# Hybrid decoder step: when the first recurrent weight blocks are loaded, when the last head's sums are prepared, and at which point the gates stand

## The chip, the cores and the metric

The kernel runs on one core of a Trainium2 chip. The metric is the device time of one execution in microseconds (us). Engines are named as in the profile: PE (TensorE matmul), PEld (its weight loads), DVE (VectorE), ACT (ScalarE), POOL (GpSimd), SP (SyncE, which here only issues DMAs).

## What is computed

One layer of a decoder for 512 prompt rows and 8 samples of 8 rows, 576 rows in all, of width 2048, in float32:

```
mod = silu(c) @ w_ada + b_ada                      # six vectors of 2048 for each condition
hn = rmsnorm(x, g1) * (1 + sc1) + sh1
q, k, v, xl, gl = split(hn @ w_in)                 # 8 heads of 128; xl, gl of 1024
attn = stick_breaking(q, k, v, bias)               # samples also over 8 cached pages of 128 keys each
xc = causal_conv4(xl)
r, i = sigmoid(xc @ w_a + b_a), sigmoid(xc @ w_x + b_x)    # 8 diagonal blocks of 128
a = exp(-8 * r * softplus(-lam)); h[t] = a[t] * h[t-1] + sqrt(1 - a[t]^2) * i[t] * xc[t]
x = x + gt1 * (concat(attn, h * gelu(gl)) @ w_out)
x = x + gt2 * conv_ffn(rmsnorm(x, g2) * (1 + sc2) + sh2)   # w_up 2048x12288, conv 3, gelu, w_down
```

Stick-breaking weights are exp(log_sigmoid(z) + sum of log_sigmoid(-z) over the later keys). Each sample attends to its own 8 new rows and to its 1024 cached rows.

## The kernel before

Everything stands transposed, features on the partitions and the 576 rows along the free dimension, as two halves of 288. Each float32 weight is split into a high and a low part (`hi` on ACT, `lo` on DVE), and a product of one **weight block** (1024 input rows by 128 output columns, 512 KB) is 48 matmuls of 288 columns (L713). Blocks pass through four slots `raw`, `w_hi`, `w_lo`: SP loads `raw` (`load`, L494), ACT makes `w_hi` (L1218), DVE `w_lo` (L1692), PE uses them. Each engine's program is one fixed list; the engines meet only by counters (`wait_ge`), so an instruction that waits holds up all behind it on its engine. The same is so on SP, whose DMAs are issued in order: a load that waits for its buffer keeps back all later ones.

The layer runs in stages:

- **Heads.** For head i, PE makes q, k and v in six block products. Between them stand five **modulation chunks** (`ada_chunk`, SP's L556, PE's L729: 1 MB of `w_ada` in two DMAs through the ring `ada_q`, whose slots come free as PE uses the chunk two before) and the work of the head before: `scores` (L809), `sums` (the sums over later keys, L821 and L826), `turn_kv`, and `weigh` (the product with the values, L843). The logits go through ACT (Abs, Exp, Ln) and DVE; `sums` needs their softplus `sp_` split again, into `high` by ACT (`sums_high`, L1275) and `low` by DVE (`sums_low`, L1789, into memory that the profile calls `ops`).
- **First recurrent block.** `lru_block(0, 0..3)`, four block products (two for xl, two for gl), stand among the last head's `scores(NH)`, `sums(NH)` and `weigh(NH)`. Behind `sums(NH)` PE sums the samples' own keys (L1011, L1015), which waits for `self_sp_ready`: the logits of the samples against their own rows, made by DVE (L1972, semaphore `self_z`), through ACT's Abs, Exp, Ln (L1437 to L1439, semaphore `self_exp`) and back on DVE (L1982 to L1984).
- **Points.** The cached keys and values, 64 pages each of 512 KB, are worked off at 128 **points** (i, p), p from 0 to 15. A point with a key page has eight transposes (L911, L915), whose results ACT and DVE copy to SBUF (L1413 and L1925, `left_taken` and `right_taken`), and eight small matmuls (`score`, L926), which work on the page of the point before and so need its copies. A point with a value page has eight small matmuls (`weigh_page`, L959). The sixteen points of round i = 0 stand alone. In the rounds 1 to 7 they stand between the matmuls of the four products `lru_block(i, q)`, one for every two of the eight input tiles.
- **Gates.** In round i, PE makes the gates of recurrence i - 1 (`gates(i - 1)`, L895: two matmuls for r, two for i). Both pass through the PSUM banks 0 and 1, which the products of xl and gl use too. So PE first waits for gl (`gl_out`, ACT's Gelu L1378), makes r, does a point, waits until ACT has read r (`r_taken`, Sigmoid L1384), makes i, does another point, waits until ACT has read i (`i_taken`), and begins the products. ACT then makes the coefficients (L1360, L1361), DVE `recurrence_a` (L1861 to L1864), ACT the root (L1365), DVE `recurrence_b` (two scans), and ACT may take the next xl only after that (`lru_done`).
- **Output projection and feed-forward.** PE takes 16 + 16 blocks of `w_out`, 48 tiles of `w_up` (L1113) and 8 groups of `w_down` (L713).

In what order SP, ACT and DVE reach these steps is written out by hand: SP in the loop over b (`ada_chunk`, then `qkv_block(b + LEAD)` with LEAD = 6), ACT and DVE in loops `for p in range(16)` with `if p == ...`. POOL loads the pages through four buffers.

In head 7 (the last), SP's loop has no more q, k and v blocks to load, and the first block of the recurrent products is issued after all five modulation chunks.

## Time and profile before

| what | value |
|---|---|
| median of 3 runs | 3016.62 us (3013.79 to 3017.61) |
| the profiled execution | 3015.11 us, its span 3013.3 us |
| PE busy | 2880.0 us, 96% of the span |
| PEld busy | 2726.0 us, 90% |
| DVE, ACT, POOL busy | 59%, 40%, 10% |
| mean granted TensorE clock | 0.982 of full speed |
| heads | up to about 580 us of the span |
| first recurrent block | about 580 to 632 us |
| points of round 0; rounds 1 to 7 | about 632 to 667 us; 667 to 1020 us |
| output projection; feed-forward | to about 1270 us; to the end |

A line of the profile names the source line, the engine, the operation and what it writes and reads. "Idle" in square brackets is the time in which the engine stood before that instruction, with what ended it. Times of a timeline count from the first instruction. The granted clock is a share of TensorE's full 2.4 GHz; 0.50 is its lower level, 1.2 GHz.

### The profile page before, as it was taken

What the parts mean: (1) busy time and instruction counts of PE and PEld (TensorE: products, weight loads), DVE (VectorE), ACT (ScalarE), POOL (GpSimd) and SP (SyncE); (2) the same over time, 40 slices, a digit from 0 to 9 for tenths busy, and PEclk for the clock granted to TensorE, in tenths of its full rate; (3) what the DMA queues carried; (4) which work ended last, traced back from release to release, by engine and by line L of the source; (5) the groups of instructions that cost most, each with busy time, mean ns of one, the idle gap of its engine ahead of it and who ended that gap; (6) DMA issues with size and microseconds to landing.
All of it is one profiled execution on the core that took longest, in us unless ns stands there. A gap on an engine that the chain in (4) does not pass through costs nothing.

```text
span 3013.3 us, 60900 instructions
## 1 busy us (share of the span) xinstructions
PE 2880.0 (96%) x24110; PEld 2726.0 (90%) x24110; DVE 1764.5 (59%) x2738; ACT 1216.5 (40%) x1481; POOL 293.6 (10%) x545
## 2 busy tenths in 40 slices
PE   6799999879999999969999999999999999999999
PEld 2499999868888899869999999999999999999999
DVE  0433343344444432398888888888888755555553
ACT  1345555444444421254444444444444422222222
POOL 0000000011212100011111111111111100000000
PEclk9799999989999999979999999999999999999999
DMA  9966555455766697523333333333333633333323
GB/s 336 338 168 171 162 162 141 141 160 177 228 201 212 191 250 220 143 69 111 103 112 104 113 109 97 111 109 111 111 95 114 206 108 108 103 106 107 105 81 107
DMA packets 608837, 444.53 MB, mean 148 GB/s; under 512 B 14553, under 2 KB 556111, under 8 KB 607453
## 3 DMA queue, kind: packets, MB, share of 16 engines
q1 hardware_dynamic: 584630, 353.39, 40.2%
q0 software_dynamic: 23904, 84.15, 8.9%
q10 hardware_dynamic: 144, 4.72, 0.4%
q8 instruction: 118, 1.93, 0.3%
q14 instruction: 41, 0.34, 0.0%
HBM read 408.14 MB, written 34.06 MB: 147 GB/s over the span
## 4 chain that ended last, share of the span: by engine, by line
PE 86%; DVE 5%; ACT 4%; DMA 3%; issue 1%; SPq 0%; POOL 0%; ACTq 0%; DVEq 0%; POOLq 0%
PE ps L713 40%; PE ps L1113 35%; PE ps L729 2%; DMA wide<-in_w_ada_dram 2%; PE ps L911 1%; PE ps L926 1%; PE ps L791 1%; DMA ada_o<-in_w_ada_dram 1%; PE ps L809 1%; PE ps L737 1%; PE ps L959 1%; PE ps L763 1%; PE ps L843 1%; PE ps L915 1%; ACT w_hi L1218 1%
## 5 line engine op out<-in xcount | busy, mean ns | idle before, releaser
L1113 PE MATMUL ps<-ops,w_hi 128*128 128x288 f32 x4608 | 920.4, 296 | 1.5 <-DVE w_lo L2076 1.5
L1113 PEld LDWEIGHTS ps<-ops,w_hi 128*128 128x128 f32 x4608 | 742.0, 189 | 1.7 <-DVE w_lo L2076 1.7
L1113 PE MATMUL ps<-ops,w_lo 128*128 128x288 f32 x2304 | 679.5, 295 | 0.0
L1692 DVE TENSOR_TENSOR w_lo<-raw,w_hi 128x1024 fp32r<-128x1024 f32 x240 | 294.0, 1225 | 647.6 <-ACT w_hi L1218 646.5
L713 PE MATMUL ps<-gs,w_hi 128*128 128x288 f32 x3072 | 534.0, 296 | 0.0
L1218 ACT ACTIVATE w_hi<-raw 128x1024 fp32r<-128x1024 f32 x240 | 253.6, 1057 | 679.1 <-PE ps L713 649.9
L713 PEld LDWEIGHTS ps<-gs,w_hi 128*128 128x128 f32 x3072 | 452.4, 189 | 0.0
L1113 PEld LDWEIGHTS ps<-ops,w_lo 128*128 128x128 f32 x2304 | 437.9, 190 | 0.0
L713 PE MATMUL ps<-act_hi,w_hi 128*128 128x288 f32 x1792 | 403.4, 307 | 18.4 <-DVE act_lo L1756 13.5
L713 PE MATMUL ps<-act_hi,w_lo 128*128 128x288 f32 x1792 | 385.1, 297 | 0.0
L713 PE MATMUL ps<-act_lo,w_hi 128*128 128x288 f32 x1792 | 384.7, 297 | 0.0
L713 PE MATMUL ps<-gs,w_lo 128*128 128x288 f32 x1536 | 329.1, 296 | 0.0
L713 PEld LDWEIGHTS ps<-act_hi,w_hi 128*128 128x128 f32 x1792 | 286.7, 190 | 44.4 <-issue 29.9
L713 PEld LDWEIGHTS ps<-act_lo,w_hi 128*128 128x128 f32 x1792 | 290.4, 190 | 0.0
L713 PEld LDWEIGHTS ps<-act_hi,w_lo 128*128 128x128 f32 x1792 | 290.1, 190 | 0.0
L1520 ACT ACTIVATE w_hi<-ax 128x1024 fp32r<-128x1024 f32 x144 | 152.9, 1061 | 260.4 <-PE ps L1113 254.7
L713 PEld LDWEIGHTS ps<-gs,w_lo 128*128 128x128 f32 x1536 | 247.6, 189 | 0.0
L2076 DVE TENSOR_TENSOR w_lo<-raw,w_hi 128x1024 fp32r<-128x1024 f32 x168 | 205.5, 1223 | 53.4 <-ACT w_hi L1520 53.3
L1520 ACT ACTIVATE w_hi<-raw 128x1024 fp32r<-128x1024 f32 x168 | 177.4, 1057 | 109.2 <-PE ps L1113 105.0
L2076 DVE TENSOR_TENSOR w_lo<-ax,w_hi 128x1024 fp32r<-128x1024 f32 x144 | 175.7, 1220 | 31.9 <-ACT w_hi L1520 31.9
L1113 PE MATMUL ps<-op,w_hi 128*128 128x288 f32 x768 | 157.5, 300 | 29.1 <-DVE ops L2168 29.1
L2212 DVE SCALAR_TENSOR_TENSOR uc<-up,vec,uc 128x592 f32<-128x592 f32 x192 | 159.9, 833 | 12.7 <-DVE uc L2212 6.4
(353 smaller groups left out, 3218.4 us busy)
## 6 DMA issues: line engine op xcount, KB each, us to landing
raw<-in_w_up_dram SPq DMA_DIRECT2D x120, 512.0 KB, 4.3
raw<-in_w_down_dram SPq DMA_DIRECT2D x128, 384.0 KB, 3.3
raw<-in_w_in_dram SPq DMA_DIRECT2D x80, 512.0 KB, 4.5
ada_q<-in_w_ada_dram SPq DMA_DIRECT2D x80, 512.0 KB, 5.4
wide<-in_w_ada_dram SPq DMA_DIRECT2D x32, 1024.0 KB, 11.2
page<-in_cache_k_dram POOLq DMA_DIRECT2D x64, 512.0 KB, 4.6
page<-in_cache_v_dram POOLq DMA_DIRECT2D x64, 512.0 KB, 4.5
ada_o<-in_w_ada_dram SPq DMA_DIRECT2D x48, 512.0 KB, 6.5
```

What stands on the lines that cost most here:

```text
L713: mm = pe.matmul(out[:, h, :], w[s][:, kk, :], x[:, row, h * HALF:(h + 1) * HALF], start=first and kk == kks[0] and w is w_hi and x is hi, ...
L729: mm = pe.matmul(ps[32 * j:32 * j + CW, bank, R0:R0 + P], cs[:, h * KB + kk, :], ring[:, slot, kk, :], start=False, stop=h == 1 and kk >= ...
L737: mm = pe.matmul(ps[:, bank, 448 + CB * j:448 + CB * (j + 1)], rows[:, j, :], sel[:], start=True, stop=True)
L763: mm = pe.matmul(ps[:, 1 + h, 0:HALF], neg_ones, sq[:, k % 2, h * HALF:(h + 1) * HALF], start=first, stop=last)
L791: mm = pe.matmul(ps[32 * j:32 * j + CW, bank, :], cs[:, WK * q + j, :], wide[:, (b + 4) % WIDE, j, :], start=q == 0, stop=q == 3, skip_gro ...
L809: pe.matmul(ps[:, b, c:c + QW[j]], kf[:, j * P:(j + 1) * P], qf[:, j * P:SEQ], start=True, stop=True)
L1113: mm = pe.matmul(ps[:, bank, 0:HALF], w[slot][:, kk, :], moving(i, kk, low), start=i not in ADDED and kk == 0 and w is w_hi and not low, s ...
L1218: act.activation(w_hi[s][:], raw[s][:], ACT.Copy).then_inc(hi_done, 1)
L1520: act.activation(w_hi[n % SLOTS if isinstance(n, int) else (7 * jj + i) % SLOTS][:], weight(j, jj, i)[:], ACT.Copy) \
L1692: dve.tensor_tensor(w_lo[s][:], raw[s][:], w_hi[s][:].bitcast(F32), ALU.subtract).then_inc(lo_done, 1)
L2076: dve.tensor_tensor(w_lo[slot][:], weight(j, jj, i)[:], w_hi[slot][:].bitcast(F32), ALU.subtract).then_inc(lo_done, 1)
L2212: dve.scalar_tensor_tensor(uc[which][:], up[which][:, w:w + SEQ + NB * 10], col, uc[which][:], ALU.mult, ALU.add).then_inc(done, 1)
```

## The change

Three things are written in another place; no instruction is added or taken out.

1. SP: the blocks 0 to 5 of the recurrent products (those of `lru_block(0, 0..3)` and two of `lru_block(1, ...)`) are loaded in the loop over b, each behind the modulation chunk of its b, as the q, k and v blocks are; blocks 6 and 7 follow, and the loop begins at i = 2.
2. The last head: ACT's `sums_high(NH)` stands behind `take_v(NH)`, ahead of `hi(u, 5)` and of the Abs, Exp, Ln of the samples' own keys; DVE's `sums_low(NH)` stands right behind the instruction that signals `self_z`, ahead of `lo(u, 5)` and of the rest of that chain.
3. Gates: in each round i of 1 to 7, PE does points 0 and 1, then gate r, point 2, gate i, point 3, and the first product has two points inside, after its fourth and sixth input tile. ACT takes the gates at p = 2 and 3, and DVE's `recurrence_a` comes at p = 4.

```
--- before.py
+++ after.py
@@ sync engine: weight blocks and modulation chunks
+            def lru_block(n):
+                i, k = n // 4, n % 4
+                load(turn(B_LRU, i, 4), k, wi_v, KB * (k % 2), KB, 128 * i + 3072 + 1024 * (k // 2))
             for b in range(LEAD):
                 qkv_block(b)
             sp.wait_ge(sem("x_turned"), KT)
...
                 if b + LEAD < 6 * NH:
                     qkv_block(b + LEAD)
+                else:
+                    lru_block(b + LEAD - 6 * NH)
+
+            for n in range(LEAD, 8):
+                lru_block(n)
 
             def lru(i):
...
-            turns(sp, NL, lru)
+            with sp.Fori(2, NL) as i:
+                lru(i)
@@ tensor engine: points inside a recurrent block's product
                 def between(kk):
-                    if kk in (2, 4, 6) and points:
-                        point(i, points[kk // 2 - 1])
+                    if kk in (6, 4, 2)[:len(points)]:
+                        point(i, points[len(points) - 1 - (6, 4, 2).index(kk)])
@@ tensor engine: gates
                 gate(i, 0, "r_mm")
-                point(i + 1, 1)
+                point(*((i + 1, 2) if i + 1 < NL else (NL, 0)))
                 if i + 1 < NL:
                     pe.wait_ge(sem("r_taken"), i + 1)
                 gate(i, 1, "i_mm")
...
             for i in range(1, NL):
                 point(i, 0)
+                point(i, 1)
                 gates(i - 1)
-                point(i, 2)
+                point(i, 3)
                 pe.wait_ge(sem("i_taken"), i)
-                lru_block(i, 0, (3, 4, 5))
+                lru_block(i, 0, (4, 5))
                 lru_block(i, 1, (6, 7, 8))
@@ scalar engine
             take_v(NH)
+            sums_high(NH)
             hi(u, 5)
...
             act.activation(wsl, wsl, ACT.Ln, bias=1.0).then_inc(sem("self_exp"), 1)
-            sums_high(NH)
             hi(u, 6)
...
-                    if p in (1, 2):
-                        take_gate(i - 1, p - 1)
+                    if p in (2, 3):
+                        take_gate(i - 1, p - 2)
@@ vector engine
                                      ALU.mult, ALU.add).then_inc(sem("self_z"), 1)
+            sums_low(NH)
             lo(u, 5)
...
             dve.tensor_tensor(z3, wsl.rearrange("p (h q) -> p h q", q=SAMP), same3, ALU.mult).then_inc(sem("self_sp_ready"), 1)
-            sums_low(NH)
             dve.memset(xlp[:, 0:3], 0.0)
...
-                    if p == 3:
+                    if p == 4:
                         recurrence_a(i)
```

The order of the instructions shows this at three places. On SP, in the last head and the first recurrent block (L556 is a modulation chunk's half, L494 a weight block), before:

```order
L494 DMA raw<-in_w_in_dram 128x8x128 x2
L556 DMA ada_q<-in_w_ada_dram 128x8x128 x10
L494 DMA raw<-in_w_in_dram 128x8x128 x4
L87 UNCONDITIONAL_BRANCH
L87 ISA
```

and now:

```order
L556 DMA ada_q<-in_w_ada_dram 128x8x128 x2
L494 DMA raw<-in_w_in_dram 128x8x128
L556 DMA ada_q<-in_w_ada_dram 128x8x128 x2
L494 DMA raw<-in_w_in_dram 128x8x128 x4
L586 UNCONDITIONAL_BRANCH
L586 ISA
```

The first two rows of the new piece are the last of four such pairs. Each of the first blocks moved ahead of the modulation chunks that used to stand before it.

On ACT, from the last head's values to its weights (`high` is `sums_high`, the `La` rows are the samples' own keys), before:

```order
L1293 ACTIVATE vn<-ps 128x512
L1218 ACTIVATE w_hi<-raw 128x1024
L1437 ACTIVATE La<-X 64x512
L1438 ACT_TABLE_LOAD
L1438 ACTIVATE La<-La 64x512
L1439 ACT_TABLE_LOAD
L1439 ACTIVATE La<-La 64x512
L1275 ACTIVATE high<-X 128x1280
```

and now:

```order
L1303 ACTIVATE vn<-ps 128x512
L1285 ACTIVATE high<-X 128x1280
L1228 ACTIVATE w_hi<-raw 128x1024
L1448 ACTIVATE La<-X 64x512
L1449 ACT_TABLE_LOAD
L1449 ACTIVATE La<-La 64x512
L1450 ACT_TABLE_LOAD
L1450 ACTIVATE La<-La 64x512
```

`high` moved ahead of a weight block and of the three steps of the own keys.

On PE, at the head of round 1 (xc, wg are the gates; kt is a `score`; page a transpose of a key page), before:

```order
L915 MATMUL ps<-ident,page 128x128 x4
L895 MATMUL ps<-xc,wg 128x288 x2
L926 MATMUL ps<-kt,X 32x128 x8
L911 MATMUL ps<-ident,page 128x128 x4
L915 MATMUL ps<-ident,page 128x128 x4
L895 MATMUL ps<-xc,wg 128x288 x2
L926 MATMUL ps<-kt,X 32x128 x8
L911 MATMUL ps<-ident,page 128x128 x4
L915 MATMUL ps<-ident,page 128x128 x4
L713 MATMUL ps<-act_hi,w_hi 128x288 x2
```

and now:

```order
L924 MATMUL ps<-ident,page 128x128 x4
L935 MATMUL ps<-kt,X 32x128 x8
L920 MATMUL ps<-ident,page 128x128 x4
L924 MATMUL ps<-ident,page 128x128 x4
L904 MATMUL ps<-xc,wg 128x288 x2
L935 MATMUL ps<-kt,X 32x128 x8
L920 MATMUL ps<-ident,page 128x128 x4
L924 MATMUL ps<-ident,page 128x128 x4
L904 MATMUL ps<-xc,wg 128x288 x2
L935 MATMUL ps<-kt,X 32x128 x8
L920 MATMUL ps<-ident,page 128x128 x4
L924 MATMUL ps<-ident,page 128x128 x4
```

Both gates moved behind one more point, and the product (L722 in the new program) begins behind the last row.

## Rows read from the trace of the kernel before

**Rows 1.** Page: the chain that ended last, by engine

```profile
PE 86%; DVE 5%; ACT 4%; DMA 3%; issue 1%; SPq 0%; POOL 0%; ACTq 0%; DVEq 0%; POOLq 0%
```

**Rows 2.** PE's waits, whole span: waiter, releaser: total us, times, longest

```profile
PE ps L895 <- ACT La L1384: 12.4, 7, 5.4
...
PE ps L821 <- DVE ops L1789: 12.1, 2, 6.9
...
PE ps L926 <- DVE kt L1925: 6.7, 7, 1.3
...
PE ps L809 <- DVE mod L1697: 2.7, 1, 2.7
...
PE ps L895 <- ACT gg L1378: 1.7, 6, 0.4
```

**Rows 3.** The chain in order of time: start us, us, what

```profile
460.20 2.16 PE ps L843 x8
...
515.24 2.16 PE ps L843 x8
...
546.37 7.11 DMA raw<-in_w_in_dram
...
577.91 2.17 PE ps L843 x8
```

**Rows 4.** SP's timeline in the last head: start us, us, what was issued

```profile
498.99 47.33 SPq L556 DMA_DIRECT2D ada_q<-in_w_ada_dram  x10
```

**Rows 5.** ACT's and DVE's timelines, the last head's sums and the own keys

```profile
609.28 0.64 ACT L1437 ACTIVATE La<-X 64x512 f32<-64x512 f32 x1 [3.55 <-DVE X L1972]
...
613.71 1.25 ACT L1275 ACTIVATE high<-X 128x1280 fp32r<-128x1280 f32 x1
...
606.44 0.90 DVE L1783 TENSOR_TENSOR X<-X,before 128x128 f32<-128x128 f32 x4
...
615.34 0.68 DVE L1984 TENSOR_TENSOR X<-La,same 64x512 f32<-64x512 f32 x1
615.95 1.48 DVE L1789 TENSOR_TENSOR ops<-X,high 128x1280 fp32r<-128x1280 f32 x1
...
625.29 0.90 DVE L1804 TENSOR_TENSOR X<-X,before 128x128 f32<-128x128 f32 x4 [1.34 <-ACT X L1287]
```

**Rows 6.** PE's timeline of the same stretch

```profile
617.57 0.76 PE L821 MATMUL ps<-high,neg_later 128*128 128x512 f32 x1 [6.93 <-DVE ops L1789]
...
621.87 0.43 PE L1011 MATMUL ps<-neg_ones,X 128*32 128x1 f32 x32
...
629.71 2.32 PE L843 MATMUL ps<-X,vn 128*128 128x512 f32 x8
```

**Rows 7.** Stretches: us, busy (instructions) by engine, granted clock, DMA share, GB/s

```profile
592.00:597.00 5.00, 5.00 (x14) 3.15 (x13) 0.72 (x2) 0.00 (x0) 0.00 (x0) 0.52 0.35 105
645.00:668.00 23.00, 21.07 (x325) 15.97 (x318) 9.37 (x14) 7.62 (x13) 6.88 (x13) 1.00 0.82 282
879.60:884.70 5.10, 5.08 (x84) 3.83 (x84) 0.00 (x0) 1.19 (x2) 0.00 (x0) 0.67 0.80 259
```

**Rows 8.** PE's timeline: second gate (L895) of rounds 1 to 5, one score (L926)

```profile
676.51 2.29 PE L895 MATMUL ps<-xc,wg 128*128 128x288 f32 x4 [5.44 <-ACT La L1384]
...
732.11 1.24 PE L895 MATMUL ps<-xc,wg 128*128 128x288 f32 x4 [1.70 <-ACT La L1384]
...
780.26 1.24 PE L895 MATMUL ps<-xc,wg 128*128 128x288 f32 x4 [1.37 <-ACT La L1384]
...
827.64 1.24 PE L895 MATMUL ps<-xc,wg 128*128 128x288 f32 x4 [0.16 <-ACT La L1384]
...
839.64 0.43 PE L926 MATMUL ps<-kt,X 128*32 128x128 f32 x8 [0.87 <-DVE kt L1925]
...
879.62 1.90 PE L895 MATMUL ps<-xc,wg 128*128 128x288 f32 x4 [1.86 <-ACT La L1384]
```

**Rows 9.** ACT's timeline, rounds 1 and 3

```profile
674.42 1.28 ACT L1384 ACT_TABLE_LOAD   x1
...
776.62 0.59 ACT L1417 ACTIVATE wT<-ps 128x512 f32<-128x512 f32 x1
```

More of the change, by code:

```diff
@@ L572, in _ @@
                     qkv_block(b + LEAD)
+                else:
+                    lru_block(b + LEAD - 6 * NH)
+            for n in range(LEAD, 8):
+                lru_block(n)
             def lru(i):
@@ L577, in lru @@
                 tile(u, 2, wi_v, 128 * i + 4096)
-            turns(sp, NL, lru)
+            with sp.Fori(2, NL) as i:
+                lru(i)
             def out_block(b):
@@ L900, in between @@
                 def between(kk):
-                    if kk in (2, 4, 6) and points:
-                        point(i, points[kk // 2 - 1])
+                    if kk in (6, 4, 2)[:len(points)]:
+                        point(i, points[len(points) - 1 - (6, 4, 2).index(kk)])
                 product(turn(B_LRU, i, 4), q, gps[0], act_hi, act_lo, first=q % 2 == 0, last=q % 2 == 1, k0=KB * (q % 2),
@@ L1027, in gates @@
                 gate(i, 0, "r_mm")
-                point(i + 1, 1)
+                point(*((i + 1, 2) if i + 1 < NL else (NL, 0)))
                 if i + 1 < NL:
@@ L1036, in _ @@
                 point(i, 0)
+                point(i, 1)
                 gates(i - 1)
[L1038 removed]
+                point(i, 3)
                 pe.wait_ge(sem("i_taken"), i)
[L1040 removed]
+                lru_block(i, 0, (4, 5))
                 lru_block(i, 1, (6, 7, 8))
@@ L1432, in _ @@
             take_v(NH)
+            sums_high(NH)
             hi(u, 5)
@@ L1439, in _ @@
             act.activation(wsl, wsl, ACT.Ln, bias=1.0).then_inc(sem("self_exp"), 1)
-            sums_high(NH)
             hi(u, 6)
@@ L1973, in _ @@
                                      ALU.mult, ALU.add).then_inc(sem("self_z"), 1)
+            sums_low(NH)
             lo(u, 5)
```

12 lines of the change are left out of this document (6 added, 6 removed).

## The prediction

> **What bounds the kernel now.** First the shares of the chain that ended last: PE holds 86% of it [rows 1]. So nothing is won by making ACT, DVE or a transfer shorter as such; only time in which PE stands, or runs at its lower clock, can be got back. The second view is PE's own waits over the whole span [rows 2]. Those that the change can touch are these: L895 (the gates) on ACT's La, 12.4 us in 7 times; L821 (the sums) on DVE's L1789, 12.1 us in 2; L926 (scores) on DVE's kt, 6.7 us in 7. The third is the chain in order of time [rows 3], where a period shows that a head is late. The last is the granted clock of short stretches [rows 7]: after a wait of some us PE works for a while at 1.2 GHz instead of 2.4, so a wait costs more than its own length.
>
> All three edits lie before 1020 us of the span, in code that each engine runs as a fixed list. What stands behind (output projection, feed-forward) waits for no clock time of its own, and I let it shift as it is.
>
> **Part 1, the first recurrent blocks.** `weigh` (L843) of one head follows that of the head before by 515.24 - 460.20 = 55.04 us, and in the last head by 577.91 - 515.24 = 62.67 us [rows 3]. The difference is 7.6 us. Its cause: SP spends 47.33 us, from 498.99 on, in ten halves of modulation chunks [rows 4], the last of which waits for PE to free a slot, and only then, at 546.37, issues the first recurrent block, which lands 7.11 us later [rows 3]. ACT's `sums_high` stands behind `hi` of that block, DVE's `sums_low` behind it, PE's sums behind that: the shorter of the two L821 waits, 12.1 - 6.9 = 5.2 us [rows 2]. The other 2.4 us are the lower clock afterwards. With the change SP's order in this head is that of the head before, so the period should be 55.04 too. What is moved costs SP's queue nothing that PE sees: a block now waits on DVE's counter ahead of the next modulation chunk, exactly as a q, k or v block does in the other heads, and PE shows no wait for a chunk of `ada_q`. What is late next: nothing, by the pattern of the head before. **7.6 us**; the lower end is the bare wait, 5.2.
>
> **Part 2, the last head's sums.** PE stands 6.93 us before L821 at 617.57 [rows 6], that is from 610.6 on. DVE finishes `sp_` at 606.44 + 0.90 = 607.3, but ACT copies it to `high` only at 613.71, behind the own keys' chain, and DVE's 1.48 us come at 615.95 [rows 5]. With the change ACT copies from 607.4 to 608.7 (1.25 us, rows 5), DVE does its part when it has signalled `self_z` (ACT's start at 609.28 dates that) and is done at about 610.8, so PE's wait is all but gone. But right behind these sums PE needs `self_sp_ready`. That comes from the own keys' chain, which runs from 609.28 to L1984's end at 616.0 [rows 5]; ACT now starts it one weight block later, about 0.3 us, so it ends at 616.3. **So a new wait takes the place of the old one**: the sums need at most 621.87 - 617.57 = 4.3 us, PE is through by 615.1 at the latest (some 1.4 us sooner at full clock) and stands until 616.4. L1011 comes at 616.4 instead of 621.87 [rows 6]. `weigh` was 629.71 - 621.87 = 7.8 us later, so 624.2; it also needs `w_ready`, at 625.29 + 0.90 = 626.2 before [rows 5]. DVE's list up to it is 1.5 us shorter by the moved L1789 and 0.3 later: 625.0 to 625.1. So `weigh` starts at 625.1 instead of 629.71: 4.6 us.
>
> From this goes a price for the clock. PE now stands about 2.7 us in front of L1011. The nearest row is a wait of just that length (L809, 2.7 us [rows 2]), and behind it the clock was 0.52 over 5 us [rows 7], which is 5 x 0.48 = 2.4 us lost. Of those, 625.1 - 624.2 = 0.9 are under the wait for `w_ready`. I take the clock as lowered: 4.6 - 1.5 = **3.1 us**; the ends are 3.1 and 4.6.
>
> **Part 3, the gates.** PE's order is the same in the seven rounds, what stands late is not. A key point takes PE about 1.5 us at full clock, a value point 0.6.
>
> - Round 1: PE stands 5.44 us before the second gate [rows 8]. ACT is in the softplus of sixteen pages until 674.42, then loads a table, does La (ends 676.5) and only then copies kt [rows 9]. Now the copy for point 1 stands ahead of the table load, at 674.4 to 675.0, and PE does point 2 from there while ACT makes La. It starts again at 675.05 instead of 676.51: 1.5 us. The gate's own wait is covered by point 2, which at the lower clock takes PE 3 us.
> - Round 2: a wait of 1.70 [rows 8], now with point 2 (1.5) in it. But point 3 holds values, 0.6 us, and ACT's second sigmoid takes 0.3 longer than that: 1.70 - 0.2 - 0.35 = 1.15.
> - Round 3: 1.37 [rows 8], and 0.4 for gl. Here point 1 follows the turning of weights at point 0, and its transposes need ACT's copy wT, done at 776.62 + 0.59 = 777.2 [rows 9], so PE stands there about 0.9 instead, and then 0.85 for La. Gain 0.35.
> - Rounds 4 and 6: 0.16 for La [rows 8] and 0.17 for gl each, all covered now: 0.6 together.
> - Round 5: 1.86, and the gate takes 1.90 instead of 1.24 us [rows 8], because the clock falls: over 5.1 us it is 0.67 [rows 7], 1.6 us lost. The wait is split in two of about 0.8 (the copy wT; the sums that DVE takes from PSUM), each shorter than those after which the clock stayed (1.70). Gain 0.6 + 1.6 = 2.2.
> - Round 7: what the seven La waits leave, 12.4 - 5.4 - 1.7 - 1.4 - 0.3 - 1.9 = 1.7, and 0.4 for gl; four value points, as uncovered as in round 3: 0.5.
> - DVE's `recurrence_a` used to keep the copy of point 4 back, and PE waited for it at 839.64, 0.87 us [rows 8]. It stands behind that copy now. This holds for rounds 4 and 6; in round 1 it is the sixteen pages' sums that kept a copy back, and they start earlier. 3 x 0.9 = 2.7 of the 6.7 us [rows 2].
>
> The sum is 1.5 + 1.15 + 0.35 + 0.6 + 2.2 + 0.5 + 2.7 = **9.0 us**. What could be late next is `lru_done`, on which ACT's take of xl hangs: but `recurrence_b` starts behind DVE's copy of point 7, at the same place of PE's products as before, so its deadline does not move. Bounds: 4 us (what the two direct effects, rounds 1 and 2 and the copies, give with half of it lost to new waits) and 11.
>
> **A rule weighed.** At the stretch of round 0, where PE does nothing but transposes and small matmuls, the clock is 1.00 over 23 us [rows 7]. The Trainium skill says otherwise (TensorE: Matmul & The Clock Gate, Part 4: PE-mode transpose): transposes do not count as PE activity as other matmuls do, and the full clock does not engage for them. By the row, standing three or four points together costs nothing; by the rule it is a rival, below. The trace speaks against the rule.
>
> **The rivals.**
>
> - A. The gates' waits only move. ACT's list is unchanged in length, and every score or transpose of points 1 to 3 hangs on an ACT copy behind a table load. For it: rounds 3 and 7, where I find the same waits again under other names. Against: rounds 1 and 2, where real work fills them. Part 3 would give 1 us: 3016.6 - 7.6 - 3.1 - 1 = 3004.9.
> - B. The clock falls at other places. It fell behind waits of 1.86 [rows 8] and 2.7 us [rows 2] and stayed behind one of 1.70 [rows 8]; the waits shift by 8 to 20 us and may meet it differently. Each fall costs or returns about 2.4 us: 2991 to 3002 around the forecast; two falls more give 3001.6.
> - C. Slower. In the seven rounds PE now does points 0 to 3 and two gates in one piece, 5 to 7 us without a product. If the clock falls in such a piece and stays low as long as it did in rows 7 (5 us), each round loses 2.4 to 3 us, and the low clock runs on into the product. That decides once it happens in every round and lasts double: 7 x 5 = 35 us against 20 gained, 3032. Below four rounds in seven it is no loss. The 1.00 of round 0 speaks against it, and that PE in the old order too did three points and two gates in a piece of 5 us, where the clock fell only behind waits. By the Trainium skill's rule weighed above it would be so.
> - D. The change doesn't do what it says on SP: the blocks are early but the chunks come late, PE waits for `ada_q` once or twice for 2 to 3 us. Part 1 would give 4: 3000.4. The head before has the same order, with its transfers competing in the same way, and no such wait; its 55.04 us [rows 3] contain it.
>
> **How the numbers follow.** 7.6 + 3.1 + 9.0 = 19.7 us. The profiled execution took 3015.11 us, its span 3013.3; it would take 2995.4, with a span of 2993.6. The median of the runs shown is 1.5 us above it, so the forecast for the median is 3016.6 - 19.7 = 2996.9. Chances: the forecast with its own bounds, B within them, 0.78; A 0.12; D 0.05; C 0.02; something else without gain 0.03. The bounds of the parts give 5.2 + 3.1 + 4 = 12.3 to 7.6 + 4.6 + 11 = 23.2, so 2993.4 to 3004.3; with one fall of the clock more or less, and 1 us for the scatter of runs, and not the whole of each at once: 2991.0 to 3004.0. A's middle lies just outside, its better half inside. This kernel's measurement can tell 0.2%, 6 us, from no change: faster means below 3010.6, and the cases above it are C and the rest: faster 0.94, same 0.04, slower 0.02.
>
> **What would show each step.** Part 1: no wait before the last head's first L821, and 55 us between its `weigh` and that of the head before. Part 2: the wait before the second L821 under 0.5 us, a new one of 2 to 3 us before L1011, `self_sp_ready` as releaser, and a clock near 0.5 behind it; if the clock stays 1.00 there, add 1.5 us of gain. Part 3: gate waits for La of 2 to 3 us in all instead of 12.4; new waits for wT or kt before points 1 and 2 in rounds 1, 3, 5 and 7; waits of L926 for kt down from 6.7 to about 4; clock 1.00 in round 5. Wrong I would be by new waits of PE on `ada_q`, by a clock under 0.9 in rounds 2 to 7, or by a different time of the feed-forward, which should stay within 1 us.

## The result, and the profile after

| | before | after |
|---|---|---|
| median | 3015.3 us (4 runs, 3013.79 to 3017.61) | 2989.74 us (4 runs, 2988.73 to 2990.45) |
| the profiled execution | 3015.11 us, span 3013.3 | 2988.73 us, span 2987.0 |
| mean granted clock | 0.982 | 0.982 |

The ratio is 0.9917, with a 95% interval of 0.9905 to 0.9929: the kernel is 25.6 us faster. The forecast was 19.7 us and 2996.9 us, with a range from 2991.0. The measured median lies 1.3 us outside.

All lines below L713 stand some lines lower in the kernel after: L713 is L722 there, L809 L818, L821 L830, L843 L852, L895 L904, L911 L920, L926 L935, L1011 L1020; on ACT L1370 is L1380 and L1384 L1394. First the chain that ended last, by engine [rows 1]:

```profile
PE 88%; DVE 5%; ACT 3%; DMA 2%; issue 1%; SPq 0%; POOL 0%; ACTq 0%; DVEq 0%; POOLq 0%
```

PE's share of it is two per cent larger. Next PE's waits between 440 and 1030 us of the span (waiter, releaser: total us, times, longest), which answer to [rows 2]:

```profile
PE ps L935 <- ACT kt L1423: 7.3, 3, 3.6
PE ps L935 <- DVE kt L1935: 4.5, 6, 1.3
...
PE ps L818 <- DVE mod L1707: 2.7, 1, 2.7
PE ps L1020 <- DVE X L1995: 2.5, 1, 2.5
PE ps L920 <- ACT wT L1427: 2.0, 2, 1.0
PE ps L904 <- ACT La L1394: 1.3, 2, 0.8
PE ps L968 <- ACT wT L1427: 1.0, 1, 1.0
PE ps L961 <- DVE psp L1928: 0.8, 1, 0.8
...
PE ps L722 <- ACT Lb L1394: 0.5, 2, 0.3
...
PE ps L830 <- DVE ops L1799: 0.2, 1, 0.2
```

The gates' wait for La fell from 12.4 us to 1.3, that of the sums for DVE's `sp_` from 12.1 to 0.2, that of the scores for DVE's kt from 6.7 to 4.5. New are the wait before L1020 (2.5), the one for ACT's kt in round 1 (3.3 of the 7.3; the 3.6 stood there before), and the small ones for wT and psp. The chain in order of time (start us, us, what) is the view of [rows 3]:

```profile
514.57 2.16 PE ps L852 x8
...
569.61 2.17 PE ps L852 x8
...
607.12 0.43 PE ps L1020 x32
...
618.21 2.17 PE ps L852 x8
```

569.61 - 514.57 = 55.04 us is now the last head's period too. Then the granted clock of some stretches (us, busy and instructions by engine, clock, DMA share, GB/s), the view of [rows 7]:

```profile
584.00:587.00 3.00, 3.00 (x9) 1.86 (x7) 0.00 (x0) 0.00 (x0) 0.00 (x0) 0.50 0.62 175
...
607.20:614.80 7.60, 7.60 (x58) 6.06 (x59) 6.28 (x12) 1.18 (x1) 0.00 (x0) 0.55 0.17 49
...
628.00:632.00 4.00, 4.00 (x37) 2.96 (x38) 1.22 (x2) 0.60 (x1) 0.53 (x1) 0.57 0.47 135
...
662.00:665.50 3.50, 3.50 (x23) 2.68 (x12) 1.42 (x2) 1.98 (x3) 0.53 (x1) 0.54 0.03 11
666.00:900.00 234.00, 227.75 (x2624) 196.81 (x2617) 112.45 (x193) 106.71 (x141) 49.36 (x95) 1.00 0.68 212
```

Each of the first four stretches is at or near the lower level (1.2 GHz), and each stands behind a wait: of 2.69 us for mod, 2.53 before L1020, 3.61 for ACT's kt in round 0, and 3.32 in round 1. Between 666 and 900 us the clock is never lowered, though PE now does points 0 to 3 and two gates in one piece in each of these rounds.

**A ruler.** To see where the time went I cut each trace at places that stand in every kernel: the first L843 (`weigh`) of head 6, of head 7 and of the last head (the own keys), and ACT's first take of the recurrent input of rounds 1 to 7. Two of these takes, of the kernel before:

```profile
706.31 0.41 ACT L1370 ACTIVATE xlp<-ps 128x288 f32<-128x288 f32 x1 [3.01 <-DVE X L1886]
...
1002.00 0.41 ACT L1370 ACTIVATE xlp<-ps 128x288 f32<-128x288 f32 x1 [7.59 <-PE ps L713]
```

and of the kernel after:

```profile
689.09 0.41 ACT L1380 ACTIVATE xlp<-ps 128x288 f32<-128x288 f32 x1 [3.00 <-DVE X L1896]
...
976.42 0.41 ACT L1380 ACTIVATE xlp<-ps 128x288 f32<-128x288 f32 x1 [7.59 <-PE ps L722]
```

Rounds 2 to 7 took 1002.00 - 706.31 = 295.7 us and take 287.3. The same cuts through the traces of both kernels and of the parts (us; "rest" is what stands behind the last take):

| kernel (trace) | head 6 to 7 | own keys | rounds 0, 1 | rounds 2 to 7 | rest |
|---|---|---|---|---|---|
| before | 62.7 | 52.0 | 76.6 | 295.7 | 2011.3 |
| before, again (e5) | 62.2 | 50.4 | 75.3 | 294.1 | 2012.7 |
| part 1 alone (e1) | 55.0 | 56.3 | 75.5 | 295.7 | 2011.2 |
| part 1 alone, again (e15) | 55.0 | 52.3 | 75.1 | 294.1 | 2010.6 |
| part 2 alone (e2) | 63.1 | 47.9 | 77.0 | 295.6 | 2016.0 |
| part 3 alone (e3) | 61.2 | 50.9 | 72.0 | 287.3 | 2010.8 |
| after | 55.0 | 48.6 | 71.0 | 287.3 | 2010.6 |
| after, again (e4) | 55.0 | 46.7 | 72.8 | 287.4 | 2014.3 |
| after, again (e14) | 55.0 | 48.7 | 74.2 | 287.4 | 2014.2 |
| recurrence at point 3 (e9) | 55.0 | 46.7 | 71.1 | 287.4 | 2012.1 |

### The profile page after: what moved, and what is told of

Same layout as the page of the kernel before. It is cut to its first block, busy times and chain, and to the rows that moved or that the text cites. A ratio compares the mean times of both kernels' runs of the same rounds, so it can differ in the third digit from the quotient of the medians.

```text
span 2987.0 us, 60886 instructions
## 1 busy us (share of the span) xinstructions
PE 2868.4 (96%) x24110; PEld 2717.9 (91%) x24110; DVE 1763.6 (59%) x2738; ACT 1217.1 (41%) x1481; POOL 294.0 (10%) x545
## 3 DMA queue, kind: packets, MB, share of 16 engines
q8 instruction: 118, 1.93, 0.3%
## 4 chain that ended last, share of the span: by engine, by line
PE 88%; DVE 5%; ACT 3%; DMA 2%; issue 1%; SPq 0%; POOL 0%; ACTq 0%; DVEq 0%; POOLq 0%
PE ps L722 42%; PE ps L1123 35%; PE ps L738 2%; DMA wide<-in_w_ada_dram 2%; PE ps L920 1%; PE ps L935 1%; PE ps L800 1%; PE ps L746 1%; PE ps L818 1%; PE ps L924 1%; PE ps L772 1%; PE ps L852 1%; PE ps L968 1%; ACT w_hi L1228 1%; DVE w_lo L1702 0%
## 5 line engine op out<-in xcount | busy, mean ns | idle before, releaser
L722 PE MATMUL ps<-gs,w_hi 128*128 128x288 f32 x3072 | 533.8, 296 | 0.0
L722 PEld LDWEIGHTS ps<-gs,w_hi 128*128 128x128 f32 x3072 | 452.3, 189 | 0.0
L722 PE MATMUL ps<-act_hi,w_hi 128*128 128x288 f32 x1792 | 402.1, 306 | 20.9 <-DVE act_lo L1766 16.1
L722 PE MATMUL ps<-act_hi,w_lo 128*128 128x288 f32 x1792 | 384.4, 296 | 0.0
L722 PE MATMUL ps<-act_lo,w_hi 128*128 128x288 f32 x1792 | 384.2, 296 | 0.0
L722 PEld LDWEIGHTS ps<-act_hi,w_hi 128*128 128x128 f32 x1792 | 286.1, 190 | 47.9 <-issue 31.3
L722 PE MATMUL ps<-gs,w_lo 128*128 128x288 f32 x1536 | 328.9, 296 | 0.0
L722 PEld LDWEIGHTS ps<-act_lo,w_hi 128*128 128x128 f32 x1792 | 289.6, 189 | 0.0
L722 PEld LDWEIGHTS ps<-act_hi,w_lo 128*128 128x128 f32 x1792 | 289.3, 189 | 0.0
L722 PEld LDWEIGHTS ps<-gs,w_lo 128*128 128x128 f32 x1536 | 247.5, 189 | 0.0
```

The source lines that it names most:

```text
L722: mm = pe.matmul(out[:, h, :], w[s][:, kk, :], x[:, row, h * HALF:(h + 1) * HALF], start=first and kk == kks[0] and w is w_hi and x is hi, ...
```

## The experiments

### The parts apart (e1 to e4)

e1 has only this part of the change (and SP's list of the later pairs from 2 on):

```diff
                 if b + LEAD < 6 * NH:
                     qkv_block(b + LEAD)
+                else:
+                    lru_block(b + LEAD - 6 * NH)
+
+            for n in range(LEAD, 8):
+                lru_block(n)
```

> The kernel before with part 1 alone (SyncE brings the first eight recurrent weight blocks between the last modulation chunks). Theory 1 (each part is worth the waits that it removes, and what is beyond them comes from shorter stretches at the low clock after the waits that stay, which depend on when those waits fall): 7.6 us up to the scores of head 7, and then 0 to 3 us more or less from the low stretches at the samples' own keys and in rounds 0 and 1. Against 3015.3 us that is 3004.7 to 3010.7, with the low stretches behind the waits at L926 changed in length though no line there was edited. Theory 2 (the gain beyond the forecast is made by the edited lines themselves, in the rounds): 3007.7 us within 0.7 us, and the rounds as long as before.

e2 has only this, and the same for `sums_low` on DVE:

```diff
             take_v(NH)
+            sums_high(NH)
             hi(u, 5)
...
-            sums_high(NH)
             hi(u, 6)
```

> The kernel before with part 2 alone (the last head's sums ahead of the samples' own keys on ScalarE and VectorE). Theory 1: 2.5 us as read between the two traces (3.1 forecast), with 0 to 3 us more or less from the low stretches of rounds 0 and 1, whose waits come 2.5 us earlier: 3009.8 to 3015.8 us. Theory 2: 3012.8 us within 0.7 us. In both the wait of 2.5 us before the samples' own sums (L1011) stands in it.

e3 has only this, with `take_gate` and `recurrence_a` one point later:

```diff
                 point(i, 0)
+                point(i, 1)
                 gates(i - 1)
-                point(i, 2)
+                point(i, 3)
                 pe.wait_ge(sem("i_taken"), i)
-                lru_block(i, 0, (3, 4, 5))
+                lru_block(i, 0, (4, 5))
```

> The kernel before with part 3 alone (gates one point later, and what goes with it). Theory 2 (the edited lines of the rounds are worth the 12.1 us by which rounds 1 to 7 grew shorter between the two traces, among others because a weight product is interrupted once less in each round): 12 us or more, 3002.0 to 3003.5 us. Theory 1 (9.0 us by the waits, and the rest from a low stretch in round 1 that is short only because parts 1 and 2 moved it): 9.0 us, about 3006.3 us, and round 1 shows the long low stretch of 6 us that it has before.

e4 is the changed kernel.

> The changed kernel again, beside the three parts on the same chip. Measured before: 2989.7 us against 3015.3, 25.6 us less. If the parts add up (theory 2), the three runs above give the same sum within 1.5 us; by theory 1 their sum may lie 1.5 to 5 us beside it, because each low stretch is another one in each kernel.

| kernel | median, runs | ratio to before (95%) |
|---|---|---|
| before, same chip | 3012.14, 22 (3007.47 to 3019.01) | |
| e1 | 3009.3, 10 (3002.71 to 3011.07) | 0.9986 (0.9977 to 0.9996) |
| e2 | 3008.6, 10 (3005.6 to 3016.49) | 0.9988 (0.9978 to 0.9998) |
| e3 | 3003.03, 7 (2998.48 to 3007.95) | 0.9967 (0.9954 to 0.9979) |
| e4 | 2992.69, 4 (2987.96 to 2993.96) | 0.9928 (0.9912 to 0.9945) |

Against what was expected, the medians settle little. e1 is 2.8 us shorter (1.2 to 6.9 by its interval), less than the 7.6 that both theories had for the head alone; its trace has the head's 7.6 us, and own keys of 56.3. e2 is 3.5 us shorter (2.5 expected by the traces, 3.1 by the forecast). e3 is 9.1 us shorter (6.3 to 13.9): that is the 9.0 of theory 1, and the 12 of theory 2 isn't excluded.

Two things follow. First, one kernel spreads over 12 us from one execution to the next; the four runs of the first comparison did not show that. Second, rounds 2 to 7 of e3 take 287.3 us, those of the changed kernel 287.3, and 287.4: what part 3 does there is the edit's own, and it is more than the forecast's 6.6. Rounds 0 and 1 of e3 (72.0) also have the shorter time without parts 1 and 2, which speaks against my theory that these had moved a low stretch away. So theory 2 is right for the rounds. The medians of the parts add up to 2.8 + 3.5 + 9.1 = 15.5 us against 19.4 for all, the means of the same runs to 4.4 + 3.6 + 10.1 = 18.1 against 21.2; with intervals of some 3 us on each, that is no proof that they don't add.

### Chance within one kernel (e5, e15)

e5 is the kernel before, e15 that of e1, both unchanged, for second traces.

> The kernel before once more, for a second trace of it. The first trace has 486.9 us from the weighing of head 6 (515.1) to the last recurrent input taken (1002.0), and 2011.3 us from there to the end. Theory 1 (the length of the stretches at the low clock is chance, within a kernel too): rounds 2 to 7 take 295.7 us again within 0.1, since the clock does not fall there, and the difference lies at the samples' own keys, in rounds 0 and 1, at the start and around 1290 us, up to 3 us each. Theory 2 (the stretches belong to the kernel): every stretch is the same within 0.5 us.

> The kernel of e1_part1_alone for a second trace. There the samples' own keys (weighing of head 7 to weighing of the last head) took 56.3 us against 52.0 and 50.4 in two traces of the kernel before, with 17 us of low clock behind L1011's place. If this is chance, it is 50 to 53 us now. If part 1 without part 2 brings it (the last modulation chunks and the sums' wait come closer together), it is 55 to 57 again, which would explain why the parts do not add up.

e5 took 3012.24 us, a run of the kernel before beside it 3017.93; e15 took 3004.23. Round 5 of the kernel before had a stretch at 0.67 [rows 7]. In e5 the same products, at the same waits, run at full clock:

```profile
877.10:882.20 5.10, 5.10 (x98) 4.41 (x99) 0.48 (x4) 1.63 (x6) 0.54 (x1) 1.00 0.78 248
```

That is the whole difference of rounds 2 to 7: 295.7 - 294.1 = 1.6 us, and the other five rounds agree within 0.05. So chance reaches into rounds 2 to 7 of this kernel, which both theories had excluded: round 5 took 51.5 us in three traces without part 3 (before, e1, e2) and 49.9 in two (e5, e15). e1 and e15 show it at the own keys. First the stretch 602 to 622 us of e1, then of e15:

```profile
602.00:622.00 20.00, 14.38 (x86) 12.47 (x87) 12.73 (x26) 7.14 (x7) 0.00 (x0) 0.57 0.22 62
```

```profile
602.00:622.00 20.00, 13.37 (x110) 12.07 (x109) 14.81 (x35) 9.76 (x10) 2.43 (x6) 0.83 0.34 88
```

PE waited 6.9 us before the sums in e1 and 6.6 in e15, and 2.7 for mod in both. At nearly the same waits the clock was 0.57 once and 0.83 once, and the own keys took 56.3 and 52.3 us. In these traces the length of a low stretch is not fixed by the kernel. e15's own keys lie where chance was expected (50 to 53). But two traces don't exclude that part 1 alone makes the own keys longer: they took 56.3 and 52.3 us with it, 52.0, 50.4 and 50.9 without parts 1 and 2 (before, e5, e3), and e1's median gained 2.8 us where its head gained 7.6. That stays open.

The rest, behind all edits, varies too, from 2010.6 to 2016.0 us. This is 1280 to 1335 us of the kernel before (rest 2011.3), then of e2 (rest 2016.0):

```profile
1280.00:1335.00 55.00, 29.46 (x150) 26.92 (x151) 51.39 (x87) 33.51 (x59) 5.14 (x8) 0.70 0.18 50
```

```profile
1280.00:1335.00 55.00, 31.29 (x141) 28.66 (x142) 50.96 (x85) 33.29 (x57) 4.56 (x8) 0.63 0.18 51
```

The clock differs, but it is no price here: PE stands for almost half of these 55 us, mostly waiting for DVE. From the first product of `w_up` on (it starts at 1289.0 and 1288.2 us) the two traces take 1724.3 and 1726.5 us, which is 2.2 of the 4.7 us and stays unexplained. The other 2.5 lie ahead of it, where e2 waited 1.93 us for a chunk of `w_ada` at 1054 us and ran at clock 0.57 over the next 8 us; the kernel before had 1.00 at that place.

### How much of the 25.6 us is the kernel's (e14)

> The changed kernel, for its time over more executions: open is how much of the 25.6 us of the first comparison (4 runs of each) is the kernel's and how much the chance of the stretches at the low clock. From the traces: the parts that repeat give 23 to 24 us (up to head 7: 7.2; own keys 4.4; rounds 0 and 1: 4.1; rounds 2 to 7: 8.0). If that is right, the difference of the medians is 23 us within 1.5, about 2990.5 us against 3013.5. If 25.6 stands: 2988.5 and less; if the forecast's 19.7 was right and the rest chance: 2993.5 and more.

2991.77 us as a median of 5 (2987.75 to 2995.62), against 3011.48 of 9; ratio 0.9926 (0.9912 to 0.9939), 19.7 us: less than the 23 within 1.5 that I expected, and by chance the forecast's own number. All executions together: 13 of the changed kernel (2987.75 to 2995.62, mean 2991.0), 44 of the kernel before (3007.47 to 3019.01, mean 3013.4). The difference of the means is 22.5 us, from the scatters (2.4 and 3.2 us) within 1.6. So some 3 of the 25.6 us are what chance in the two first samples can give; e14 by itself lies as far on the other side.

### What the interruption of a product costs (e6, e7)

In e6 point 3 goes back into the product, in rounds 2 to 7:

```diff
-                point(i, 3)
+                if i == 1:
+                    point(i, 3)
                 pe.wait_ge(sem("i_taken"), i)
-                lru_block(i, 0, (4, 5))
+                lru_block(i, 0, (4, 5) if i == 1 else (3, 4, 5))
```

> The changed kernel, but in rounds 2 to 7 point 3 stands again inside the weight block's product (three points in it, as before the change) instead of ahead of it. If the 1.8 us by which rounds 2 to 7 won more than forecast (8.36 against 6.6) come from one interruption of a product fewer in each round, each of these rounds gets 0.15 to 0.3 us longer than in the changed kernel (48.29, 46.57, 50.01, 49.12, 50.01, 43.33), 1 to 1.8 us in all. If an interruption costs nothing, they stay within 0.05 us, unless a wait for ScalarE's copy of the gate shows (L920 or the product behind it), which would then be read as a wait.

Rounds 2 to 7 took 293.2 us, 5.9 more than in the changed kernel. Most of it is a wait, as PE's timeline of round 4 shows (idle time in square brackets), of e6:

```profile
863.91 1.14 PE L904 MATMUL ps<-xc,wg 128*128 128x288 f32 x4
865.88 0.53 PE L722 MATMUL ps<-act_hi,w_hi 128*128 128x288 f32 x2 [0.83 <-ACT Lb L1395]
```

and of the changed kernel:

```profile
861.52 1.14 PE L904 MATMUL ps<-xc,wg 128*128 128x288 f32 x4
862.59 0.64 PE L935 MATMUL ps<-kt,X 128*32 128x128 f32 x16
863.16 0.66 PE L920 MATMUL ps<-ident,page 128*128 128x128 f32 x4
863.66 0.60 PE L924 MATMUL ps<-ident,page 128*128 128x128 f32 x4
864.01 0.52 PE L722 MATMUL ps<-act_hi,w_hi 128*128 128x288 f32 x2
```

ACT's sigmoid of the second gate takes 0.83 us that nothing covers now, six times 0.83 = 5.0 us, of which the changed kernel has 0.5; PE's other waits in rounds 2 to 7 are the same to 0.1 us. (The expectation had named such a wait, but not counted it in its 1 to 1.8 us.) The 5.9 - 4.5 = 1.4 us that are left are the interruption: the same work, no wait, one more break in the product. They are 0.23 a round, 0.19 to 0.28 in each of the six. e7 measures it from the other side. In the last round it sets the first two value points of the last three products at one place:

```diff
                 def between(kk):
+                    if i == NL - 1 and q:
+                        if kk == 4:
+                            point(i, points[0])
+                            point(i, points[1])
+                        if kk == 6:
+                            point(i, points[2])
+                        return
```

> The changed kernel, but in the last round (i = 7) the first two value points of each of the last three weight products stand at one place (3 interruptions fewer, the same work). If resuming a product behind a point costs 0.17 us, the last round (to the first recurrent input taken 43.33 us) and what follows up to the last gates get shorter by 0.5 us in all. If an interruption costs nothing: no difference over 0.05 us, or longer where two pages in a row wait for their DMA.

The last round up to its take was 43.01 us instead of 43.33 with one join, and from there to the last gates 18.52 instead of 19.16 with two: 0.32 us a join, 0.95 in all (forecast: 0.5). PE's timeline with a join, in e7:

```profile
970.02 1.08 PE L975 MATMUL ps<-page,wT 128*32 128x128 f32 x32
971.03 0.53 PE L722 MATMUL ps<-act_hi,w_hi 128*128 128x288 f32 x2
971.40 0.42 PE L722 MATMUL ps<-act_lo,w_hi 128*128 128x288 f32 x2
...
972.46 0.42 PE L722 MATMUL ps<-act_hi,w_lo 128*128 128x288 f32 x2
972.81 0.65 PE L975 MATMUL ps<-page,wT 128*32 128x128 f32 x16
973.38 0.53 PE L722 MATMUL ps<-act_hi,w_hi 128*128 128x288 f32 x2
```

Two pages in a row hold the product up for 1.01 us, one for 973.38 - 972.81 = 0.57, so the second saves 0.13. The rest is the product's: by the same timeline the first pair of matmuls behind a page takes 0.37 us to the next instead of 0.26, and the page follows the last pair after 0.35. The change itself takes one interruption out of each round.

### The recurrence's place on DVE (e9)

```diff
-                    if p == 4:
+                    if p == 3:
                         recurrence_a(i)
```

> The changed kernel, but VectorE starts the recurrence at point 3 again, as before the change, instead of at point 4. The forecast puts 2.7 us on key copies of VectorE that no longer stand behind it. If that term is right, rounds 1 to 7 (to the inputs taken at 689.1 and 976.4 us in the changed kernel) get 1.5 to 2.7 us longer, in rounds 4 and 6 by about 0.9 us each (the wait of 0.87 us at 839.64 in the kernel before), with L935 waiting for VectorE's kt there. If the gates' later place alone took those waits away, the rounds stay within 0.1 us.

No change: rounds 2 to 7 take 287.4 us, round by round within 0.03 of the changed kernel, rounds 0 and 1 71.1 instead of 71.0, and PE's waits of e9 have the same row as the changed kernel's:

```profile
PE ps L935 <- DVE kt L1935: 4.5, 6, 1.3
```

PE's waits for the copies of rounds 4 and 6 (0.87 us each before, 0.18 now) shrank without the recurrence's move; the gates' later place is the only other edit of part 3.

### A better kernel (e8, e10 to e13)

e8 moves the own keys' sums on PE into the middle of round 0's last product, and on DVE the last head's weights ahead of the taps:

```diff
-            pe.wait_ge(sem("self_sp_ready"), 1)
+            def self_sums(kk):
+                if kk != 4:
+                    return
+                pe.wait_ge(sem("self_sp_ready"), 1)
...
-            lru_block(0, 3)
+            product(turn(B_LRU, 0, 4), 3, gps[0], act_hi, act_lo, first=False, last=True, k0=KB, between=self_sums)
```

> The changed kernel with the samples' own sums on TensorE moved from ahead of the last weight product of round 0 to its middle, and VectorE's part of the last head's weights ahead of the taps. If the wait of 2.53 us there (L1020, for VectorE's L1995) and the low clock behind it are what part 2 of the change leaves on the table: the weighing of the last head starts at about 612 instead of 618.0 us, with no wait over 0.3 us before the sums, and the kernel is 4 to 6 us shorter than the changed one. If something else sets the weighing (ScalarE's exponential of the weights, L1297 at 613.62): it stays at 615 or later, and 0 to 3 us are won.

PE's timeline and the clock of the stretch in e8:

```profile
606.96 0.43 PE L1023 MATMUL ps<-neg_ones,X 128*32 128x1 f32 x32
...
611.62 2.32 PE L852 MATMUL ps<-X,vn 128*128 128x512 f32 x8
```

```profile
601.00:612.00 11.00, 11.00 (x103) 9.72 (x103) 9.40 (x28) 6.50 (x7) 0.92 (x3) 1.00 0.32 83
```

No wait, full clock, and `weigh` at 611.62: the own keys take 43.2 us instead of 46.7 to 48.7, and the kernel 2986.35 us in one execution (the changed kernel's mean is 2991.0). e8 tests both moves together, not each by itself.

e10 joins, in every product of rounds 1 to 7 with three points, the first two at one place where one of them is a value page:

```diff
+                joined = i and len(points) == 3 and (key_page(i, points[0]) is None or key_page(i, points[1]) is None)
...
+                    if joined:
+                        for p in {3: points[:2], 6: points[2:]}.get(kk, ()):
+                            point(i, p)
```

> The changed kernel, but in rounds 1 to 7 the first two of the three points in a weight product stand at one place wherever at least one of them is a value page. In the last round a join was worth 0.31 us (three of them 0.95 us). Rounds 1 to 7 have 18 such products or so (3 each in rounds 2, 3, 5 and 7, fewer in the others). If each is worth 0.3 us, the kernel is 4 to 6 us shorter than the changed one. If a join of a key page with a value page only moves a wait (the copies of the key page, or a page's DMA), it is 0 to 2 us, and L935 or L968 wait longer.

It took 2990.31 us in one execution, and rounds 2 to 7 286.1 us, 1.2 less than in the changed kernel: the expectation's second case. Where the order of the points is the same, a finer ruler is PE's own: the first gate (L904) of a round to that of the next. Of round 5 in the changed kernel:

```profile
856.37 1.14 PE L904 MATMUL ps<-xc,wg 128*128 128x288 f32 x4
...
905.82 1.14 PE L904 MATMUL ps<-xc,wg 128*128 128x288 f32 x4
```

so 49.45 us. Rounds 2 to 7 take by it 47.65, 46.89, 49.69, 49.45, 49.36 and 40.40 us in the changed kernel, 48.46, 46.16, 49.71, 48.72, 49.36 and 39.45 in e10. Rounds 3 and 5 gain 0.73, that is 0.24 for each join of a key page with a value page, round 7 0.95. Rounds 4 and 6 gain nothing and round 2 loses 0.81, by waits: in PE's waits of e10 up to 1000 us these two, with other line numbers, were 4.5 and 2.0 us before the joins:

```profile
PE ps L940 <- DVE kt L1940: 5.3, 6, 2.1
PE ps L925 <- ACT wT L1432: 3.2, 2, 1.6
```

e11 adds three moves to e8, on DVE and ACT:

```diff
-            lo(u, 4)
             take_mod(5, M_QKV + 35, 4, 7 + NH)
+            lo(u, 4)
...
-            take_gl(0)
-            hi(u, 7)
...
             for p in range(16):
                 take_left(0, p)
+                if p == 4:
+                    take_gl(0)
+                if p == 7:
+                    hi(u, 7)
```

> The kernel of e8_own_sums_inside_block with three more moves: VectorE takes the last modulation chunk ahead of its half of a weight block (the wait of 2.69 us for mod gets 1.2 us shorter), ScalarE's vector c is worked out while the last weighing is waited for, and ScalarE's gate of round 0 and its weight block, and VectorE's, stand behind points 4, 7 and 8 of round 0 instead of ahead of the first (the wait of 3.6 us for ScalarE's kt goes). If these waits are paid on the path, it is 4 to 6 us shorter than e8's 2986.4 us, up to the chance of the low stretches (3 us). If the engines' work only moves (the points of round 0 then wait for copies by as much), 1.2 us.

It took 2980.09 us in one execution, 6.3 less than e8 (4 to 6 expected), of which 1.3 lie in the rest, where nothing was edited. PE's waits from 575 us on, in e11:

```profile
PE ps L920 <- DMA page<-in_cache_k_dram: 4.7, 4, 2.3
PE ps L935 <- DVE kt L1940: 3.6, 5, 1.3
PE ps L935 <- ACT kt L1426: 3.6, 2, 3.3
...
PE ps L818 <- DVE mod L1712: 1.3, 1, 1.3
```

Mod is down from 2.7 to 1.3 and the wait of 3.6 us for ACT's first kt is gone, but as much comes back as waits for pages (4.7 us, 1.1 in e8): round 0 now runs into its DMA. What is left of the gain before the rest is 3.1 us in the own keys, 1.5 in rounds 0 and 1 and 0.5 ahead of head 6's `weigh`, and single traces vary by as much.

> The kernel of e11_own_keys_reordered with the joins of e10_pages_joined_all_rounds. If the waits and the interruptions add up: 4 (e8) + 5 + 5 us less than the changed kernel's 2990 to 2993 us, 2976 to 2979 us, a ratio of 0.988 against the kernel before. If they overlap or bring new waits: 2981 to 2985 us.

> The kernel of e11_own_keys_reordered with pages joined in rounds 3, 5 and 7 alone, where e10 read a gain (0.92, 0.91 and 0.95 us; rounds 2, 4 and 6 lost 0.54, 0.19 and 0.19). Deterministic part: 284.6 us for rounds 2 to 7 (e12: 286.3), and 2.8 us less than e11 in all: about 2978 us as a median, a ratio near 0.988 against the kernel before. If the joins of e12 in rounds 1 and 2 were worth something in the first round (66.8 against 70.4 us up to the input of round 1), that stretch is 70 again and the median is above e12's 2978.4.

e12 (e11 with e10's joins) took 2978.39 us (4 runs, 2973.77 to 2981.05; ratio 0.9884, 0.9866 to 0.9902), e13 (joins in rounds 3, 5 and 7 alone) 2977.85 (4 runs, 2973.88 to 2980.96; ratio 0.988, 0.9864 to 0.9896). Both beat the changed kernel by some 13 us; they can't be told from each other. By PE's ruler e13's rounds take 47.65, 46.16, 49.70, 48.72, 49.36 and 39.43 us: all of the joins' gain, 2.4 us, and none of the loss. The 284.6 us expected by the first ruler were 285.6; the 0.19 us that it showed as lost in rounds 4 and 6 are there again with nothing joined in them, since ACT's take comes behind PE in the joined rounds and behind DVE in the others. e12's short rounds 0 and 1 (66.8 us) were 70.9 in e13; the median above e12's that was expected with it didn't come.

## Why the prediction was too small, and which of its steps failed

The direction held, and so did the mechanisms of parts 1 and 2 and of the gates' waits. The sum was short, one mechanism in it (key copies that stand behind the recurrence) was wrong, and one cost (breaking off a product) stood at nothing. The measured median lies 7.2 us below the forecast. Of these, 3.2 are the start: I subtracted from 3016.6 us, the median of three runs, and the mean of 44 is 3013.4. 2.8 are the gain, 22.5 us and not 19.7. 1.2 are that the four executions shown first lay below the mean of 13, 2991.0 us. That mean stands at the very foot of the range. By the ruler, with the means of the traces before and after (before: the traces without the part concerned; after: the kernel, e4, e14 and e9, and those of e1, e2 and e3 that have the part):

| term | forecast | traces |
|---|---|---|
| part 1, head 6 to 7 | 7.6 | 62.3 - 55.0 = 7.3 |
| part 2, own keys | 3.1 | 52.4 - 47.7 = 4.7 |
| part 3, rounds 0 and 1 | 2.4 | 75.9 - 72.2 = 3.7 |
| part 3, rounds 2 to 7 | 6.6 | 295.0 - 287.4 = 7.6 |
| rest | 0 | 2012.1 - 2012.8 = -0.7 |

The sum is 22.6 us; up to the `weigh` of head 6 the traces before and after agree within 0.2 in the mean.

**Part 1** was right, in size too: the period is 55.04 us, that of the head before, and PE shows no wait on `ada_q` there (rival D). The last head's extra time without part 1 was 7.6, 7.2, 8.1 and 6.1 us in four traces.

**Part 2** was right in its mechanism to a few tenths: the wait before the sums 0.2 us, a new one of 2.53 before L1020, released by DVE's L1995, and clock 0.55 behind it. e8, which also moves DVE's weights, suggests that the new wait and its clock are worth 3.5 to 5.5 us at this place. In the first pair of traces the own keys became 52.0 - 48.6 = 3.4 us shorter, for a forecast of 3.1, and that is partly luck: L1020 came 37.5 us behind head 7's `weigh` and not 38.5, and the low clock behind it took 3.4 us (7.6 us at 0.55) and not 2.4. What was mis-sized for the mean of 4.7 is the clock: the forecast took one length for each stretch. Behind the old wait it varied (own keys 50.4 to 56.3 us in five traces), behind the new one too (46.7 to 48.7 in five; in e4 and e9, with 46.7, the clock was back at 1.00 some 2 us sooner). So 0.4 of the 1.6 us missed are the old stretch, longer in the mean than in the one trace of it, and 1.2 the new one, shorter than priced.

**Part 3 is where the sum failed, in two terms.** The first is a cost that was put at nothing: "standing three or four points together costs nothing" was argued for the clock alone. The change also takes one interruption out of each round's first product, 0.23 us by e6, 0.32 by e7, so 1.4 to 1.9 us over rounds 2 to 7. A count of PE's waits fits that. Between the two takes shown above they were in the kernel before (waiter, releaser: total us, times, longest):

```profile
PE ps L895 <- ACT La L1384: 6.9, 6, 1.9
PE ps L926 <- DVE kt L1925: 5.0, 5, 1.3
PE ps L895 <- ACT gg L1378: 1.6, 5, 0.4
PE ps L713 <- ACT Lb L1384: 0.5, 2, 0.3
```

That is 14.0 us; between the two takes of the changed kernel it is 9.2 (3.6 for kt, 3.0 for wT, 1.3 for La, 0.8 for psp, 0.5 for Lb). So waits gave 4.8 us, and the forecast's 6.6 had 5.0 for them and 1.6 for the clock of round 5. Measured were 8.36 in the first pair: 4.8, the 1.6 of the clock, and 1.9 us without any wait or low clock, the size of six breaks. By single rounds it is less clean: these 1.9 us are 0.2 to 0.3 in rounds 3, 5 and 7, but 0.65 in 4 and 6 and -0.2 in 2, so the breaks account for the sum and not for each round. The 1.6 were luck in part: the kernel before doesn't always have the low clock of [rows 7] (three traces of five), and in the mean the rounds gained 7.6. In the sum itself, round 3's term doesn't follow from its working: 1.37 + 0.4 - 0.9 - 0.85 is 0.02 and not 0.35; its waits fell by 0.28.

The second term is the 2.7 us for DVE's copies "behind the recurrence". The sum was of the right order (PE's wait for kt fell by 2.2, from 6.7 to 4.5), the cause was wrong: e9 puts the recurrence back and loses nothing.

**Rounds 0 and 1** gave 3.7 us in the mean for a forecast of 2.4. PE's waits there were 12.6 to 13.3 us in the five traces without part 3 and 9.4 to 11.6 in the five with it, 2.7 less in the mean; the wait of 5.44 for the gate became one of 3.32 for kt, as foreseen. The other 1.0 is not settled. The traces with part 3 spread from 71.0 to 74.2 us: in the longest (e14) PE waited 2.7 us for pages instead of 0.5, and behind the wait of 3.3 us the clock fell to 0.54 over 3.5 us in the first trace and stayed at 1.00 in e9.

**The rivals.** A (the gates' waits only move, part 3 gives 1 us) is out as a whole, but it holds for much of rounds 2 to 7: there 8.5 us for La and gl became 1.3 for La and 3.8 for wT and psp. B was right in kind and too small in size: it allowed for two falls of 2.4 us, and the executions differ by 12 us. C is out: the clock was 1.00 from 666 to 900 us, with transposes, scores and gates in one piece. The Trainium skill's rule (TensorE: Matmul & The Clock Gate, Part 4: PE-mode transpose) is that transposes don't count as activity and the full clock doesn't engage for them. The trace disagrees for such mixed pieces; I looked at none of transposes alone. D is out by part 1 above.

**The range** failed at its foot. It was built from three runs within 4 us, to which I gave 1 us of scatter, and the bounds of the parts were the bare waits with a given clock. 44 executions scatter by 3.2 us around their mean. With 3.2 in place of 1 the foot would have been 2988.8, an estimate, below the measured 2989.74.

## What to carry to other kernels

Count, beside waits, how often a change makes one stream of matmuls break off for another: here a break costs 0.23 to 0.32 us without any idle time being shown, and joining two short pieces of work gains that where both are ready (in e10 other joins gained nothing, because new waits took it). Before you price a few us from one trace, take a second trace of the same kernel and cut both at the same places: pieces that don't agree need many executions, and even agreement of two is no proof (round 5's low clock stood in three traces of five). Where a wait sits ahead of work that doesn't need it (own sums ahead of a product), putting it in the middle of that work can give back the wait and the low clock behind it (3.5 to 5.5 us in e8, with DVE's weights moved too).

## What the hardware showed that I had not expected

- The same kernel at the same waits gets low stretches of different length: clock 0.67 or 1.00 over the same 5.1 us of round 5, 0.57 or 0.83 over 20 us of the own keys behind waits of 6.9 and 6.6 us. Behind the wait of 3.3 us in round 1 the clock was 0.54 once and 1.00 in e9. The whole kernel spreads over 12 us; between traces the own keys differ by up to 5.9 us at the same waits, the rest by up to 5.4, round 5 by 1.6.
- Rounds 2 to 7 of the changed order, whose longest wait is 1.3 us, repeat to 0.03 us on three chips: 48.29, 46.57, 50.01, 49.13, 50.02, 43.33 us.
- A product broken off for small matmuls and resumed pays 0.23 us (e6) to 0.32 us (e7) a break, with no idle time in the trace.
